# DeltaNet preparation: half of a unit's diagonal-block stores issued from ScalarE's queue, and the first group's blocks collected right behind the eighth unit

## What is computed

```python
decay = jnp.exp(jnp.where(incl, cum[..., :, None] - cum[..., None, :], -jnp.inf))
k_beta = k * beta[..., None]
m = jnp.where(strict, jnp.einsum('bhnid,bhnjd->bhnij', k_beta, k) * decay, 0.0)
...
sol = lax.linalg.triangular_solve(m + jnp.eye(CHUNK, dtype=m.dtype), rhs, left_side=True, lower=True,
                                  unit_diagonal=True)
...
attn = jnp.where(incl, jnp.einsum('bhnid,bhnjd->bhnij', q, k) * decay, 0.0)
```

## Time and profile before

| | us |
|---|---|
| median of 3 runs | 1727.04 (1724.84 to 1727.08) |
| the profiled execution | 1726.73 |
| its span, first to last instruction | 1724.9 |
| time outside the span | 1.8 |
| stage `dn_a`, from SyncE's first load to the next stage's first compute instructions | 511.0 to 594.7 |
| mean granted TensorE clock | 0.948 |

### The profile page before, as it was taken

The page is one execution under the profiler, slowest core; times in us unless marked ns, Lnnn a source line. Parts: engine busy times, 40 slices in busy tenths (PEclk is TensorE's granted clock), DMA queues, the critical chain, the costliest instruction groups (busy, mean ns, idle before and its releaser), DMA issues. The chain is left out here.

```text
span 1724.9 us, 21667 instructions
## 1 busy us (share of the span) xinstructions
PE 1541.6 (89%) x8270; PEld 1249.9 (72%) x8270; DVE 1214.7 (70%) x1409; ACT 919.8 (53%) x1310; POOL 304.6 (18%) x371
## 2 busy tenths in 40 slices
PE   6899999998997799999899896299999999999991
PEld 3686788787876678877377685178888888888871
DVE  4872754396656656666699655798888888888873
ACT  5441354375447376643110453177777777777753
POOL 0300410070005686000000361000100010001001
PEclk9999999998999899999999997599999999999996
DMA  9571310041018633410321443399999999999957
GB/s 346 167 267 44 133 50 1 3 153 59 7 32 241 212 94 104 129 36 1 122 98 50 161 146 120 137 368 391 375 395 397 399 384 390 397 394 387 383 212 219
DMA packets 109098, 345.13 MB, mean 200 GB/s; under 512 B 37501, under 2 KB 46998, under 8 KB 84419
## 3 DMA queue, kind: packets, MB, share of 16 engines
q1 hardware_dynamic: 99534, 320.34, 49.2%
q0 software_dynamic: 5328, 18.88, 4.6%
q10 hardware_dynamic: 4133, 4.53, 1.0%
HBM read 301.14 MB, written 37.32 MB: 196 GB/s over the span
## 5 line engine op out<-in xcount | busy, mean ns | idle before, releaser
L3721 DVE TENSOR_TENSOR w_lo<-w_raw,w_hi 128x2048 fp32r<-128x2048 f32 x192 | 438.1, 2291 | 64.0 <-ACT w_hi L3663 64.0
L3663 ACT ACTIVATE w_hi<-w_raw 128x2048 fp32r<-128x2048 f32 x192 | 368.1, 1918 | 145.4 <-PE ps L3608 132.9
L3606 PE MATMUL ps<-w_hi,xsT_hi 128*128 128x512 f32 x512 | 202.1, 395 | 1.1 <-DVE xsT_lo L3726 1.1
L3608 PE MATMUL ps<-w_hi,xsT_lo 128*128 128x512 f32 x512 | 199.8, 390 | 0.0
L3607 PE MATMUL ps<-w_lo,xsT_hi 128*128 128x512 f32 x512 | 199.5, 390 | 0.0
L3574 POOL DMA_INDIRECT moe_sum<-y,idx_col x15 | 30.3, 2020 | 461.2 <-ACT y L3683 430.2
L3606 PEld LDWEIGHTS ps<-w_hi,xsT_hi 128*128 128x128 f32 x512 | 96.3, 188 | 20.8 <-DVE xsT_lo L3726 1.5
L3608 PEld LDWEIGHTS ps<-w_hi,xsT_lo 128*128 128x128 f32 x512 | 96.1, 188 | 20.2
L3607 PEld LDWEIGHTS ps<-w_lo,xsT_hi 128*128 128x128 f32 x512 | 96.2, 188 | 19.2
L3606 PE MATMUL ps<-w_hi,hiddenT_hi 128*128 128x512 f32 x256 | 99.7, 390 | 0.6 <-DVE hiddenT_lo L3738 0.6
L3607 PE MATMUL ps<-w_lo,hiddenT_hi 128*128 128x512 f32 x256 | 99.6, 389 | 0.0
(11 more groups left out here) (619 smaller groups left out, 3643.0 us busy)
## 6 DMA issues: line engine op xcount, KB each, us to landing
w_raw<-in_moe_w_gate SPq DMA_DIRECT2D x64, 1024.0 KB, 6.8
w_raw<-in_moe_w_up SPq DMA_DIRECT2D x64, 1024.0 KB, 8.7
w_raw<-in_moe_w_down SPq DMA_DIRECT2D x64, 1024.0 KB, 9.1
w_mod_row<-in_w_mod SPq DMA_DIRECT2D x32, 512.0 KB, 4.9
w_mod<-in_w_mod SPq DMA_DIRECT2D x8, 1024.0 KB, 17.6
dn_ma<-dn_ma SPq DMA_DIRECT2D x16, 512.0 KB, 3.7
dn_mT<-dn_ma SPq DMA_DIRECT2D x20, 256.0 KB, 3.4
x_tile<-in_x SPq DMA_DIRECT2D x8, 512.0 KB, 15.7
```

The costliest lines, as they stand in the source:

```text
L3606: nc.tensor.matmul(out, h[:, kk, :], wh[w][:, c:c + 512], start=kk == 0, stop=False)
L3608: last = nc.tensor.matmul(out, l[:, kk, :], wh[w][:, c:c + 512], start=False, stop=kk == KD - 1)
L3663: nc.scalar.activation(wh[q % RING][:, :], S.raw[q % RAW][:, :], ACT.Copy).then_inc(s.hi, 1)
L3721: nc.vector.tensor_tensor(wl[q % RING][:, :], S.raw[q % RAW][:, :], wh[q % RING][:, :].bitcast(F32), ALU.subtract).then_inc(s.lo, 1)
```

## The change

Blocks 0 and 1 of a unit are still stored by SyncE; blocks 2 and 3 by ScalarE, in its iteration n for unit n - 2 and behind the load of unit n + 3, for the same units 0 to 15. In SyncE's list the first group's collection comes directly after unit 7; unit 8's blocks and tile follow it, in the same order as for the others.

```diff
-    def store_blocks(sp, n, tile, sem):
+    def store_blocks(eng, n, tile, sem, which):
 
         _, st, d, _ = U[n]
         at = st // 4 * P * 1024 + blocks_at(st, d) * 1024
-        for b in range(4):
+        for b in which:
             c = slice(DB * b, DB * b + DB)
             ap = bass.AP(tensor=A["dn_u"].tensor, offset=at + b * 1024, ap=[[DB, DB], [4096, HEADS], [1, DB]])
-            sp.dma_start(ap, tile[c, 0, :, c]).then_inc(sem, 16)
+            eng.dma_start(ap, tile[c, 0, :, c]).then_inc(sem, 16)
...
             def blocks(n):
                 sp.wait_ge(s.mt, n + 1)
-                store_blocks(sp, n, MA[n % DN_RING], ma_st[n % DN_RING])
+                store_blocks(sp, n, MA[n % DN_RING], ma_st[n % DN_RING], (0, 1))
 
             for n in range(5):
                 load(sp, n)
             for n in range(DN_GROUP):
                 blocks(n)
                 store(n)
-            store(DN_GROUP)
             collect(sp, 0)
-            blocks(DN_GROUP)
-            for n in range(DN_GROUP + 1, HEAD):
+            for n in range(DN_GROUP, HEAD):
                 blocks(n)
                 store(n)
...
                     load(nc.scalar, n + 3)
+                if 2 <= n < 2 * DN_GROUP + 2:
+                    act.wait_ge(s.mt, n - 1)
+                    store_blocks(nc.scalar, n - 2, MA[(n - 2) % DN_RING], ma_st[(n - 2) % DN_RING], (2, 3))
```

## The result

| | before | changed |
|---|---|---|
| median of 5 runs (us) | 1727.04 (1724.84 to 1728.72) | 1733.43 (1729.89 to 1735.36) |
| ratio, 95% interval | | 1.0033 (1.0022 to 1.0044) |
| profiled execution | 1726.73 | 1729.89 |
| its span | 1724.9 | 1728.1 |
| mean granted clock | 0.948 | 0.948 |

The forecast was 1727.5 with a range to 1731.2. The ratio is worth 5.7 us (0.0033 x 1727), between 3.8 and 7.6. The profiled execution shows only 3.2 more, since it reached the stage 2.2 us earlier than the one of before (first load at 508.83 against 511.04, after code that is the same). Counted so, the stage takes 89.8 us against 84.9, up to the start of the last memset with which the next stage begins.

What follows compares the result with a forecast made beforehand. SyncE's issuing looked like the stage's pace, with full DMA engines left open. TensorE's branch (+0.4) and GpSimd's (+0.1), partly overlapping, were put at +0.6 us: 1727.3 profiled, about 1727.5 at the median; range 1724.0 to 1731.2.

Steps and rivals of the forecast that it cites:

- ScalarE takes the place of SyncE as the pace: ScalarE's iterations with two added block issues: 0.86 us more a unit, so ScalarE sets the pace.
- c: ScalarE's time per unit, from Exp to Exp: 1.74 + 2p = 2.78 us, against 1.92 before.
- The collection: First group's collection on SyncE, read by GpSimd: issued at 545.2, landing in 4.2 us, GpSimd starting 0.1 us later.
- p: One block issue on ScalarE with its gap: taken as 0.52 us, between 0.35 and 0.73.
- D: Delay of TensorE's key products of unit 11, behind ScalarE's Exp and copy: 9c - 20.9 = 4.1 us.
- it shifts as a whole: From unit 11 on, the stretch paced by TensorE's gate products was to move unchanged by D, 4.1 us.
- 4.9 us of cover: VectorE's units ended 4.9 us before GpSimd's handover; with 4.1 us of delay they were still to end ahead.
- The landing of the inverse: SyncE's store of the inverse, behind its shifted last DMAs: landed at 592.8 in place of 592.41, D - 3.7 = +0.4 us.
- Rival 1: ScalarE's issues held up like SyncE's, p = 0.73 in iterations 6 to 10: +4.2 us, time 1731.2; chance 0.24.
- Rival 2: SyncE's issuing was the whole limit and ScalarE has room: collection read at 545, -4.4 us, time 1722.6; chance 0.13.
- Rival 3: DMA engines limit both kernels, only the reordering counts: collection lands after 3.7 us, -1.2, time 1725.8; chance 0.10.

Runs made afterwards that it cites:

- keep_clock: The changed kernel with nine matmuls without use on TensorE ahead of unit 11; ratio 1.0054 (1.0035 to 1.0074) against the kernel before.
- more_handed: reorder_only with GpSimd handing the first group's substitution to VectorE after 17 columns in place of 20; ratio 0.9988 (0.9977 to 0.9999) against the kernel before.
- reorder_only: The kernel before with only the first group's collection moved directly behind unit 7, all block stores still from SyncE; ratio 0.9995 (0.9981 to 1.0009).
- scalar_held_5: reorder_only with five copies that nothing reads on ScalarE behind the load in iterations 2 to 10; ratio 1.0016 (1.0004 to 1.0029) against the kernel before.

## Why the prediction was wrong

- **ScalarE takes the place of SyncE as the pace: right.** c was to be 2.78 and was 2.79 in the first profile; an issue was to take 0.52 with its gap, and the median was 0.46 without it, with one of 1.44. A hit that close is luck: the same program's second profile has 3.14, outside the 2.7 to 2.9 that were to show the step. Unit 11's key products start 0.95 us behind its Exp, as reckoned, in all kernels of the table with c above 2 except keep_clock, where the filler held them; with c at 1.9 they start 3 to 4 us behind it, since VectorE comes last there.
- **The collection: right.** Issue and landing were to give +0.1 on GpSimd's branch; it was -0.5 at the copy. (One slip: at p = 0.35 the prediction's terms put unit 7's last block at 542.7, not 542.0; nothing rests on it.)
- **D, the delay of TensorE's unit 11: 5.2 us, not 4.1.** The term 9c took a uniform pace; the pair in iteration 10 took 1.92 us. In the second profile c is 3.14, and D 6.3, where 9c - 20.9 would give 7.4.
- **The step that failed is "it shifts as a whole".** I let D pass through the stretch of gate products unchanged. It grew to 7.6 at VectorE's last unit: 1.65 in unit 11's product, which ran at the lower clock level after TensorE's idle of 4.2 us, 0.15 ahead of it, and 0.64 in the units behind. In the second profile D = 6.3 grew to 8.0, 1.2 of it in the product. TensorE's rows showed that product slowed in the kernel before already (3.5 us against 3.0 for the next), and the prediction gave its clock no term. That the product's extra time is due to the longer gap is not shown: more_handed has D = 0.3 and a product 1.15 longer, without the change's split. With 4.9 us of cover, D = 4.1 costs nothing, D = 5.2 passed through unchanged would start VectorE's part 0.2 later, and 7.6 started it 2.6 later.
- **The landing of the inverse: right in kind, much too small.** The sum had it: late transfers push its end by D - 3.7. With 4.1 that is 0.4, with 7.6 it is 3.9, and measured, from the first load, 5.1 (2.6 of it the later start, 2.5 the longer landing). The forecast had no term for two transfers of 512 KB that go out 1.1 us apart; with the collection moved away the landing took 3.3.
- **The rivals.** Rival 1 gave 1731.2, the nearest; its premise, issues held up to 0.73 us, held in the second profile and not in the first, where the loss was there already. Rival 2 is out: fewer issues on SyncE gained nothing at the collection. Rival 3's gain of the order, 1.2, was met by reorder_only's landing and by 1.0 of its stage, but the landings of 3.7 to 6.2 us with the same order leave it unshown; and it wrongly took the units' pace as set by the DMA engines: scalar_held_5 moves it with ScalarE alone. By the rule of the Trainium skill that was weighed there (page "DMA: Bandwidth & Descriptors", section "Issuing engines are not separate DMA queues") the split saves sequencer time alone. The runs agree: no gain at the collection, which went out at 33.36 against 33.46. The loss begins with the time that ScalarE gives for the issues.
- **The range** was narrow because its bounds were applied to c, and every bound then passed through the same two shifts.

## What to carry to other kernels

A DMA issue moved to an engine that computes is a piece of that engine's work: add its 0.5 us (0.73 at the median in another execution) to the engine's cycle and see whether the cycle then sets the pace; one issue fitted here, two did not. A delay that is followed through a chain has to be priced again at each engine: behind a gap on TensorE the next matmuls may run at the lower clock level (24 of them took 4.0 to 5.2 us in place of 3.0), and a transfer that goes out close behind another large one lands later. A clock level that is low in one trace may be low without your change as well, so look for it in a second profile before charging it to the change. Where one engine idles ahead of a handover, moving the handover may be the cheaper change: together with the new order three columns gave 2.1 us (0.2 to 4.0).

## What the runs showed that was not expected

- The same issue on ScalarE's queue takes 0.46 us at the median in one execution and 0.73 in another of the same program, over whole stretches.
- With four matmuls of filler in TensorE's gap, 3.8 us together at a granted clock of 0.51, the 24 matmuls behind them ran at 1.00; without them, at 0.50 to 0.56 in the changed kernel's first profile.
- TensorE's clock stood at its lower level ahead of unit 11 in executions with and without a long gap there.
- The stage behaves as if with a threshold: against the kernel before, c of 2.39 costs nothing, 2.79 costs 4.9 us, 3.75 costs 15.6.
